# Where the second half of one projection stands among the heads that it feeds: a reordered stretch of a two-block transformer kernel

## The chip, the cores and the metric

The program runs on one core of a Trainium2 chip. The metric is the device time of one execution in microseconds. Before the change it was 1682.24 us, the median of three runs (1674.70 to 1685.97 us). Engines: PE is TensorE, DVE is VectorE, ACT is ScalarE, POOL is GpSimd, SP is SyncE, which only issues transfers here.

## The reference

Two blocks follow each other on one sequence of 256 tokens of width 2048, all in fp32. The first is an attention and recurrent block with a modulated norm; the change doesn't touch it. The second mixes three branches, multiplies them by one matrix, and ends in a feed-forward part:

```python
h = rms_norm(x, g_mix[l])
z = h @ w_in[l]
z_pool, z_q, z_kv, z_kr, z_mq = jnp.split(z, IN_SPLITS_2, axis=-1)
y_pool = pool_mixer(z_pool, w_pool[l], pool_scale[l])
y_mla = mla_mixer(z_q, z_kv, z_kr, pos, ...)            # 8 heads, keys and values from a latent of 256
y_mem = memory_cross_attention(z_mq, mem, ...)          # 4 heads over 256 memory rows
x = x + jnp.concatenate([y_pool, y_mla, y_mem], axis=-1) @ w_o[l]
x = x + conv_glu_ffn(rms_norm(x, g_ffn[l]), w_gate[l], w_up[l], conv_w[l], conv_b[l], w_down[l])
```

Each of the 8 heads of `mla_mixer` takes 192 query and key columns from up-projections of the latents, norms them, rotates 64 of them, and does a causal softmax over 256 keys and the product with 128 value columns.

## The kernel before

**Blocks and halves.** Activations lie transposed, 128 features by 256 tokens to a tile. Every fp32 weight is split into two parts of fp32r: ScalarE copies the hi part (`wh`, L1366), VectorE subtracts it for the low part (`wl`, L1748). A block is one 128 x 128 piece of weight; it takes three matmuls of 256 columns (L1077 to L1079). Eight blocks are a half; its weights come as half of a 1 MB transfer into one of 4 `raw` buffers, and `wh` and `wl` have four slots each. TensorE starts a half when its low part is there (`s_lo`), and ScalarE fills a slot when the half four before is done (`s_half`). So each half costs ScalarE and VectorE one instruction of 128 x 1024.

**The order.** `plan()` lists the weight blocks as the host packs them, `order()` the same blocks with the small work between. The small work (head tasks) is given to six lanes. After each block `step()` may issue the next stage of a lane if the planner's own clocks say that its input is there; `until(...)` and `force` issue stages at once, whatever the clocks say. Every engine then runs its part of the one list in order: an instruction that waits holds up all behind it on its engine.

**Names in the stretch.** For the mla heads g is 0 (heads 0 to 3) or 1 (heads 4 to 7). `un` are the key projections, one tile a head, `uq` the query projections, `ur` the rotary parts of two heads, and `uv` the values of four heads, a tile of its own kind (`m_half`: the activations are the stationary side, L1100 to L1102, and it fills two banks). `oa`, `ob` and `o2` are the output matrix in three parts by rows: `oa` (four blocks a tile, 16 tiles) needs the cross-attention heads, `ob` (six blocks a tile) heads 0 to 3 and the pool groups 0 and 1, `o2` heads 4 to 7 and the pool groups 2 and 3. Each tile is added into `xs` by VectorE (L2166). `pz` are the pool branch's projections, which GpSimd averages (L2305 to L2313), and `pf` the small products behind them (`pool_end`, L1341, scaled by L2178).

**A head's stages**, in order: sq (squares on ScalarE, L1592 to L1598), rot (L1306), u (L2058, L2267, L2270), ss (sums of squares, L1310 to L1312), r1 (L1752), rstd (L1558, L1560), norm (L2007 to L2011, L2064, L2065 on VectorE and then L2274, L2278 on GpSimd), scores (L1235), max (L1939, L1942), exp (L1496), rc (L1945), scale (L1500), turn (L1242), pt (L1504), pv (L1246, L1248), hi (L1608), lo (L2070). Heads h and h + 4 use the same buffers, and the hook `scored` on `un`, `uq` and `ur` forces the stages of head h up to its scores before the tile of head h + 4 is copied:

```python
def scored(tile):
    h = 2 * tile[1] + 1 if tile[0] == "ur" else tile[1]
    if h >= 4:
        o.until((("mla", h - 4), "scores"))
    o.plain(tile)
```

**Banks.** Tiles take the PSUM banks 0 to 3 in turn, and the first matmul of a tile waits until the tile before it in that bank is copied or added (`bank_clear`).

**Values.** `vv` and `vx` hold 256 x 512 values each. `vx` has the cross-attention values first; before the change it also takes the values of heads 4 to 7 (L1627), once the four cross heads are through (L1631 to L1633), and the pv of a head reads `(vv, vx)[h // 4]` (L1320).

Of the kernel before, what the change touches and what calls it, by code (L numbers as in the profile page):

```python
# [14 lines left out]
P = 128  # L15
T = 256
D = 2048
KT = D // P
# [87 lines left out]
def plan():  # L106
# [46 lines left out]
    ups = []  # L153
# [21 lines left out]
    for name, kts in O2_PARTS:  # L175
        blocks = [("w_o_2", kt, (128 * j,)) for j in range(KT) for kt in kts]
        parts.append([blocks[i:i + 8] for i in range(0, len(blocks), 8)])
    line += tile_halves(128) + parts[0] + ups[1]["un"] + ups[1]["uv"] + ups[1]["uq"] + ups[1]["ur"] + tile_halves(256) + tile_halves(384)
    line += parts[1] + parts[2]
    for u in range(0, len(line), 2):  # L180
        out.append(("x", "second", line[u] + line[u + 1]))
    for j in range(FT):
# [275 lines left out]
def order():  # L458
# [256 lines left out]
    heads(0)  # L715
    pool_tile(1)
    o.until(*[("mem", j) for j in range(4)])
    o2_part(0, 0, KT)
    up(1, ("un", "uq", "ur", "uv"))
    heads(1)  # L720
    pool_end(0, o.gemm_bank())
    pool_end(1, o.gemm_bank())
    pool_tile(2)
    pool_tile(3)
    o.mix_half = o.half
    pool_end(2, o.gemm_bank())
    pool_end(3, o.gemm_bank())
    o.until(*[("mla", h) for h in range(4)])
    o2_part(1, 0, KT)
    o.until(*[("mla", h) for h in range(4, 8)])  # L730
    o2_part(2, 0, KT)
    o.o2_half = o.half
# [44 lines left out]
def program(nc, table, wts, ada, xN, xT, memN, cb, cst, vec, msk, wpool, dt, out):  # L777
    o = order()
    with ExitStack() as ctx:
# [283 lines left out]
        def _(e):  # L1063
# [234 lines left out]
            def mla(t, k):  # L1298
                h = t[1]
                s = h % 4  # L1300
                B, bank, j = lset[s], 4 + s, h // 2
                half = slice(64 * (h % 2), 64 * (h % 2) + 64)
                q, kh, qrh = qn[:, s, :], kn[:, s, :], qr[half, j % 2, :]
                if k == "rot":
                    e.wait_ge(*after(t, "act", "gr"))
                    e.matmul(ps[bank][:, 0:T], cs[half, CST["rot"][0]:CST["rot"][1]], qrh, start=True, stop=True).then_inc(mark(t, "pe", "rot"))  # L1306
                if k == "ss":
                    e.wait_ge(*after(t, "dve", "u"))
                    e.wait_ge(*after(("rk",), "act", "sq"))
                    e.matmul(ps[bank][:, :], ones[:], B["sq"], start=True, stop=False)  # L1310
                    e.matmul(ps[bank][:, 0:T], ones[half, :], B["r"][half, 0:T], start=False, stop=False)
                    e.matmul(ps[bank][:, T:512], ones[half, :], krr[half, :], start=False, stop=True).then_inc(mark(t, "pe", "ss"))  # L1312
                if k in SOFTMAX:
                    if k == "scores":
                        e.wait_ge(*after(t, "dve", "k"))
                        e.wait_ge(*after(t, "pool", "kr"))
                    if k == "pv":
                        e.wait_ge(*after(("uv", h // 4), "act", "c1"))
                    softmax(t, k, bank, [(q, kh), (qrh, B["sq"][half, 0:T])], True,
                            [(vv, vx)[h // 4][:, i, s * P:(s + 1) * P] for i in range(2)], B)  # L1320

            def cross(t, k):
                h = t[1]
# [37 lines left out]
        def _(e):  # L1361
# [262 lines left out]
                    e.activation(hB[:, 12 + h, 0:T], ps[4 + lane][:, 0:T], ACT.Copy).then_inc(mark(t, "act", "hi"))  # L1624

            def m_tile(t):
                dst = {"mk": lambda: kraw.rearrange("p (a b) -> p a b", a=2), "mv": lambda: vx, "uv": lambda: (vv, vx)[t[1]]}[t[0]]()  # L1627
                e.wait_ge(*tile_end(t))
                if t[0] in ("mk", "mv"):
                    e.wait_ge(*after(("open",), "dve", "mr4"))  # L1630
                if t == ("uv", 1):  # L1631
                    for h in range(4):
                        e.wait_ge(*after(("mem", h), "pe", "pv"))  # L1633
                banks = o.banks[t]
                for i in range(2):
                    scale = rmc[:, i:i + 1] if t[0] in ("mk", "mv") else 1.0
                    e.activation(dst[:, i, :], ps[banks[i]][:, :], ACT.Copy, scale=scale).then_inc(mark(t, "act", f"c{i}"))
# [796 lines left out]
```

## Time and profile before

| what | value |
|---|---|
| median of three runs | 1682.24 us |
| the profiled execution | 1685.97 us |
| its span, first to last instruction | 1684.2 us |
| mean granted TensorE clock | 0.981 |
| PE busy | 1605.6 us (95%) |
| DVE busy | 1171.0 us (70%) |
| ACT busy | 876.0 us (52%) |
| POOL busy | 130.6 us (8%) |
| the profile's chain that ended last | PE 77%, DVE 12%, ACT 6%, issue 3%, POOL 2% |

The span is what the profile's times refer to. Busy times of PE include modelled ends of pipelined matmuls, so one matmul's duration is longer than the distance to the next. The stretch that the change reorders lies between 757 and 890 us.

### The profile page before, as it was taken

The numbers are of one execution on the slowest core, as the hardware profiler recorded it, in microseconds if no ns is written. First come the engines' busy times: TensorE is split into PE (matmuls) and PEld (weight loads), VectorE is DVE, ScalarE is ACT, GpSimd is POOL, SyncE is SP. The second block draws the span as 40 slices with busy tenths as digits, with TensorE's granted clock in tenths as the row PEclk, the third lists the DMA queues.
The fourth block names the chain that finished last, engine by engine and source line by source line (L and its number), as shares of the span: only waits on it lengthen the run. The fifth ranks groups of instructions, "written<-read, shape, count | busy, mean of one in ns | idle before, by whom it ended". The sixth has DMA issues, their size and how long they took to land.

```text
span 1684.2 us, 25128 instructions
## 1 busy us (share of the span) xinstructions
PE 1605.6 (95%) x9962; PEld 1426.1 (85%) x9962; DVE 1171.0 (70%) x1758; ACT 876.0 (52%) x1362; POOL 130.6 (8%) x151
## 2 busy tenths in 40 slices
PE   6979899989998999988999999999999999999998
PEld 5767789988998999986899888888888888887887
DVE  4778776877676986657586777777777767556554
ACT  7654545767654555463555554444444444444442
POOL 0000000321210220022413000000000000000000
PEclk9989999999999999998999999999999999999999
DMA  8789975533455774342244455554555455555552
GB/s 323 294 336 375 349 299 197 204 113 108 175 200 196 286 276 175 128 148 76 101 145 152 166 189 178 197 191 175 185 200 178 174 198 198 177 188 187 200 177 74
DMA packets 48869, 332.14 MB, mean 197 GB/s; under 512 B 5424, under 2 KB 8880, under 8 KB 9072
## 3 DMA queue, kind: packets, MB, share of 16 engines
q1 hardware_dynamic: 48384, 328.17, 53.5%
q0 software_dynamic: 368, 2.36, 0.4%
q8 instruction: 79, 1.29, 0.3%
q14 instruction: 38, 0.31, 0.1%
HBM read 328.41 MB, written 2.10 MB: 196 GB/s over the span
## 4 chain that ended last, share of the span: by engine, by line
PE 77%; DVE 12%; ACT 6%; issue 3%; POOL 2%; DMA 0%; ACTq 0%; SPq 0%; DVEq 0%; POOLq 0%
PE ps L1081 29%; PE ps L1082 15%; PE ps L1077 7%; PE ps L1079 6%; PE ps L1078 6%; DVE wl L1748 3%; DVE raw L1784 3%; ACT wh L1366 3%; PE ps L1124 2%; PE ps L1126 2%; PE ps L1125 2%; DVE xs L2166 1%; PE ps L1160 1%; PE ps L1161 1%; PE ps L1202 1%
## 5 line engine op out<-in xcount | busy, mean ns | idle before, releaser
L1748 DVE TENSOR_TENSOR wl<-raw,wh 128x1024 fp32r<-128x1024 f32 x512 | 625.0, 1233 | 376.8 <-ACT wh L1366 375.9
L1366 ACT ACTIVATE wh<-raw 128x1024 fp32r<-128x1024 f32 x512 | 530.2, 1054 | 375.9 <-PE ps L1082 172.8
L1081 PE MATMUL ps<-hA,wh 128*128 128x512 f32 x1408 | 499.2, 400 | 0.0
L1082 PE MATMUL ps<-hA,wl 128*128 128x256 f32 x1408 | 396.2, 281 | 0.0
L1081 PEld LDWEIGHTS ps<-hA,wh 128*128 128x128 f32 x1408 | 265.3, 188 | 66.2
L1082 PEld LDWEIGHTS ps<-hA,wl 128*128 128x128 f32 x1408 | 266.7, 189 | 0.0
L1081 PE MATMUL ps<-hB,wh 128*128 128x512 f32 x704 | 250.1, 398 | 2.4 <-DVE xs L2166 1.5
L1077 PE MATMUL ps<-hA,wh 128*128 128x256 f32 x752 | 221.3, 294 | 0.0
L1078 PE MATMUL ps<-hA,wh 128*128 128x256 f32 x752 | 213.3, 284 | 0.0
L1079 PE MATMUL ps<-hA,wl 128*128 128x256 f32 x752 | 213.1, 283 | 0.0
L1082 PE MATMUL ps<-hB,wl 128*128 128x256 f32 x704 | 198.1, 281 | 0.0
L1077 PE MATMUL ps<-hB,wh 128*128 128x256 f32 x576 | 168.0, 292 | 12.4 <-DVE hB L1927 6.6
L1078 PE MATMUL ps<-hB,wh 128*128 128x256 f32 x576 | 164.4, 285 | 0.0
L1079 PE MATMUL ps<-hB,wl 128*128 128x256 f32 x576 | 164.3, 285 | 0.0
L1081 PEld LDWEIGHTS ps<-hB,wh 128*128 128x128 f32 x704 | 132.1, 188 | 37.5 <-DVE xs L2166 3.4
L1077 PEld LDWEIGHTS ps<-hA,wh 128*128 128x128 f32 x752 | 144.5, 192 | 1.8 <-issue 1.2
L1078 PEld LDWEIGHTS ps<-hA,wh 128*128 128x128 f32 x752 | 144.7, 192 | 0.8 <-issue 0.2
L1079 PEld LDWEIGHTS ps<-hA,wl 128*128 128x128 f32 x752 | 144.6, 192 | 0.0
L1082 PEld LDWEIGHTS ps<-hB,wl 128*128 128x128 f32 x704 | 132.7, 189 | 0.0
L1077 PEld LDWEIGHTS ps<-hB,wh 128*128 128x128 f32 x576 | 111.3, 193 | 17.4 <-issue 14.3
L1124 PE MATMUL ps<-wh,hA 128*128 128x512 f32 x256 | 103.3, 403 | 19.4 <-ACT xs L1543 7.1
L1078 PEld LDWEIGHTS ps<-hB,wh 128*128 128x128 f32 x576 | 111.4, 193 | 0.4 <-issue 0.2
(277 smaller groups left out, 2000.0 us busy)
## 6 DMA issues: line engine op xcount, KB each, us to landing
raw<-in_wts SPq DMA_DIRECT2D x256, 1024.0 KB, 4.8
raw<-in_ada SPq DMA_DIRECT2D x48, 1024.0 KB, 5.1
work<-in_memN SPq DMA_DIRECT2D x2, 1024.0 KB, 7.5
xs<-in_xN SPq DMA_DIRECT2D x1, 2048.0 KB, 22.2
xs<-in_xT POOLq DMA_DIRECT2D x2, 1024.0 KB, 5.7
out_T<-xs SPq DMA_DIRECT2D x16, 128.0 KB, 1.7
work<-in_cb SPq DMA_DIRECT2D x1, 1024.0 KB, 14.3
wp<-in_dt SPq DMA_DIRECT2D x8, 128.0 KB, 2.3
```

Source lines behind the costliest of these rows:

```text
L1077: e.matmul(po, w1, hl[:, 0:T], start=first, stop=False)
L1078: e.matmul(po, w1, hl[:, T:2 * T], start=False, stop=False)
L1079: i = e.matmul(po, w2, hl[:, 0:T], start=False, stop=last)
L1081: e.matmul(ps[bank][:, :], w1, hl, start=first, stop=False)
L1082: i = e.matmul(ps[bank][:, T:2 * T], w2, hl[:, 0:T], start=False, stop=last)
L1124: e.matmul(po, hi, w1, start=kt == kts[0], stop=False)
L1125: e.matmul(po, hi, w2, start=False, stop=False)
L1126: m = e.matmul(po, lo, w1, start=False, stop=kt == kts[-1])
L1160: e.matmul(po, hi, w1, start=kt == 0, stop=False)
L1366: e.activation(wh[:, h % WS, :], raw[:, n % RAW, part * HALF:(part + 1) * HALF], ACT.Copy).then_inc(s_hi)
L1748: e.tensor_tensor(wl[:, h % WS, :], src, wh[:, h % WS, :].bitcast(F32), ALU.subtract).then_inc(s_lo)
L1784: e.tensor_tensor_reduce(src, src, cbt, 1.0, 0.0, ALU.mult, ALU.add, c).then_inc(mark(t, "dve", "ttr"))
```

## The change

The second group's keys and queries (`un`, `uq`, `ur` of heads 4 to 7) come after eight of the sixteen `oa` tiles instead of after all; the other eight `oa` tiles follow, and then the second group's values (`uv` 1), after heads 0 to 3 are through. The values go into `vv`, in place of those of heads 0 to 3, and no longer into `vx`; so their copy waits for the pv of head 3 and no longer for the cross heads. The pool products `pf` 2 and 3 come behind four tiles of `ob` instead of ahead of them. The wait for heads 0 to 3 now stands ahead of `uv` 1 instead of ahead of `ob`. `plan()` packs the weights in the new order.

```diff
@@ plan()
-    line += tile_halves(128) + parts[0] + ups[1]["un"] + ups[1]["uv"] + ups[1]["uq"] + ups[1]["ur"] + tile_halves(256) + tile_halves(384)
-    line += parts[1] + parts[2]
+    line += tile_halves(128) + parts[0][:4]
+    for key in ("un", "uq", "ur"):
+        line += ups[1][key]
+    line += parts[0][4:] + ups[1]["uv"] + tile_halves(256) + tile_halves(384) + parts[1] + parts[2]
@@ order()
     o.until(*[("mem", j) for j in range(4)])
-    o2_part(0, 0, KT)
-    up(1, ("un", "uq", "ur", "uv"))
+    o2_part(0, 0, 8)
+    up(1, ("un", "uq", "ur"))
+    o2_part(0, 8, KT)
+    o.until(*[("mla", h) for h in range(4)])
+    up(1, ("uv",))
     heads(1)
     pool_end(0, o.gemm_bank())
     pool_end(1, o.gemm_bank())
     pool_tile(2)
     pool_tile(3)
     o.mix_half = o.half
+    o2_part(1, 0, 4)
     pool_end(2, o.gemm_bank())
     pool_end(3, o.gemm_bank())
-    o.until(*[("mla", h) for h in range(4)])
-    o2_part(1, 0, KT)
+    o2_part(1, 4, KT)
@@ TensorE, mla()
-                            [(vv, vx)[h // 4][:, i, s * P:(s + 1) * P] for i in range(2)], B)
+                            [vv[:, i, s * P:(s + 1) * P] for i in range(2)], B)
@@ ScalarE, m_tile()
-                dst = {"mk": lambda: kraw.rearrange("p (a b) -> p a b", a=2), "mv": lambda: vx, "uv": lambda: (vv, vx)[t[1]]}[t[0]]()
+                dst = {"mk": lambda: kraw.rearrange("p (a b) -> p a b", a=2), "mv": lambda: vx, "uv": lambda: vv}[t[0]]()
                 if t == ("uv", 1):
-                    for h in range(4):
-                        e.wait_ge(*after(("mem", h), "pe", "pv"))
+                    e.wait_ge(*after(("mla", 3), "pe", "pv"))
```

What the planner makes of it, at two places. The first is VectorE at the norms of heads 0 to 3. Before, from the norm of head 3 (its five rows from L2007 to L2065) to the start of that of head 0; `xs<-xs,ps` is the add of an `oa` tile, `wl<-raw,wh` the low part of a half:

```order
L2007 TENSOR_TENSOR ps<-work 128x512
L2009 SCALAR_TENSOR_TENSOR ps<-ps,work 128x512
L2011 SCALAR_TENSOR_TENSOR work<-ps,work 128x512
L2064 SCALAR_TENSOR_TENSOR work<-work,cols 128x256
L2065 SCALAR_TENSOR_TENSOR work<-work,vs 128x256
L2166 TENSOR_TENSOR xs<-xs,ps 128x256
L1748 TENSOR_TENSOR wl<-raw,wh 128x1024
L2166 TENSOR_TENSOR xs<-xs,ps 128x256 x2
L1748 TENSOR_TENSOR wl<-raw,wh 128x1024
L2166 TENSOR_TENSOR xs<-xs,ps 128x256
L2007 TENSOR_TENSOR ps<-work 128x512
```

Now, with lines four higher, from the low part ahead of the second pair of rotations on (r1 and the norm of head 2, and at once that of head 3):

```order
L1752 TENSOR_TENSOR wl<-raw,wh 128x1024
L2062 TENSOR_TENSOR work<-ps,cs 64x256 x2
L1756 TENSOR_SCALAR work<-ps 128x512 x2
L2011 TENSOR_TENSOR ps<-work 128x512
L2013 SCALAR_TENSOR_TENSOR ps<-ps,work 128x512
L2015 SCALAR_TENSOR_TENSOR work<-ps,work 128x512
L2068 SCALAR_TENSOR_TENSOR work<-work,cols 128x256
L2069 SCALAR_TENSOR_TENSOR work<-work,vs 128x256
L2011 TENSOR_TENSOR ps<-work 128x512
L2013 SCALAR_TENSOR_TENSOR ps<-ps,work 128x512
L2015 SCALAR_TENSOR_TENSOR work<-ps,work 128x512
```

The low parts and the adds that stood between the norms are gone from there; they follow behind the norm of head 1.

The second place is VectorE at the scaling of the pool products 2 and 3 (L2178, now L2182). Before, behind the norm of head 6:

```order
L2007 TENSOR_TENSOR ps<-work 128x512
L2009 SCALAR_TENSOR_TENSOR ps<-ps,work 128x512
L2011 SCALAR_TENSOR_TENSOR work<-ps,work 128x512
L2064 SCALAR_TENSOR_TENSOR work<-work,cols 128x256
L2065 SCALAR_TENSOR_TENSOR work<-work,vs 128x256
L1752 TENSOR_SCALAR work<-ps 128x512
L2178 TENSOR_SCALAR work<-ps,vs 128x256
```

Now, behind those of heads 4 and 7:

```order
L2011 TENSOR_TENSOR ps<-work 128x512
L2013 SCALAR_TENSOR_TENSOR ps<-ps,work 128x512
L2015 SCALAR_TENSOR_TENSOR work<-ps,work 128x512
L2068 SCALAR_TENSOR_TENSOR work<-work,cols 128x256
L2069 SCALAR_TENSOR_TENSOR work<-work,vs 128x256
L2170 TENSOR_TENSOR xs<-xs,ps 128x256
L2011 TENSOR_TENSOR ps<-work 128x512
L2013 SCALAR_TENSOR_TENSOR ps<-ps,work 128x512
L2015 SCALAR_TENSOR_TENSOR work<-ps,work 128x512
L2068 SCALAR_TENSOR_TENSOR work<-work,cols 128x256
L2069 SCALAR_TENSOR_TENSOR work<-work,vs 128x256
L2182 TENSOR_SCALAR work<-ps,vs 128x256
```

Two norms and the add of `ob` 3 stand directly ahead of the scaling, where one norm stood.

## Rows read from the trace of the kernel before

**Rows 1.** The page: busy us (share) x instructions; a group: busy us, mean ns

```profile
PE 1605.6 (95%) x9962; PEld 1426.1 (85%) x9962; DVE 1171.0 (70%) x1758; ACT 876.0 (52%) x1362; POOL 130.6 (8%) x151
L1748 DVE TENSOR_TENSOR wl<-raw,wh 128x1024 fp32r<-128x1024 f32 x512 | 625.0, 1233 | 376.8 <-ACT wh L1366 375.9
```

**Rows 2.** Windows: length, busy us (instructions) by engine, granted clock, DMA share, GB/s

```profile
771.00:778.00 7.00, 6.75 (x54) 6.21 (x52) 6.83 (x12) 3.11 (x4) 2.95 (x4) 1.00 0.28 118
778.00:786.00 8.00, 5.80 (x35) 4.31 (x35) 7.86 (x18) 2.21 (x3) 2.34 (x3) 1.00 0.39 131
786.00:801.00 15.00, 13.16 (x43) 9.77 (x44) 8.34 (x26) 6.26 (x21) 1.75 (x2) 0.54 0.00 1
...
838.00:845.00 7.00, 6.78 (x40) 5.22 (x40) 5.13 (x8) 3.44 (x6) 3.22 (x5) 1.00 0.21 44
845.00:885.00 40.00, 39.86 (x311) 37.21 (x309) 32.39 (x67) 21.09 (x44) 5.33 (x6) 1.00 0.41 151
```

**Rows 3.** Timeline of PE: start, us, instruction, [idle before <- releaser]

```profile
778.39 0.39 PE L1077 MATMUL ps<-hB,wh 128*128 128x256 f32 x1 [0.63 <-DVE xs L2166]
785.99 3.00 PE L1235 MATMUL ps<-work 128*128 128x128 f32 x8 [1.81 <-POOL work L2278]
792.40 3.20 PE L1235 MATMUL ps<-work 128*128 128x128 f32 x8 [1.84 <-POOL work L2278]
838.22 0.70 PE L1341 MATMUL ps<-work,wp 128*128 128x256 f32 x2 [1.83 <-POOL work L2313]
885.72 0.55 PE L1242 MATMUL ps<-cs,work 128*128 128x128 f32 x3 [0.86 <-ACT work L1500]
886.94 0.67 PE L1246 MATMUL ps<-work 128*128 128x256 f32 x2 [0.67 <-ACT work L1504]
888.82 0.39 PE L1077 MATMUL ps<-hB,wh 128*128 128x256 f32 x1 [0.64 <-DVE hB L2070]
```

**Rows 4.** PE's pace: chain of waits (0.12, 0.21, 0.43, 0.23) and timeline (the rest)

```profile
760.08 0.12 PE ps L1078
...
760.60 0.70 PE L1306 MATMUL ps<-work,cs 64*128 64x256 f32 x4
761.23 1.12 PE L1310 MATMUL ps<-work,ones 128*128 128x512 f32 x2
...
763.34 1.13 PE L1310 MATMUL ps<-work,ones 128*128 128x512 f32 x2
...
779.21 3.37 PE L1235 MATMUL ps<-work 128*128 128x128 f32 x16
...
796.54 0.21 PE ps L1077
...
798.88 0.43 PE ps L1101
...
800.31 0.23 PE ps L1102
```

**Rows 5.** Timeline of the other engines at a head's stages, and the pool products

```profile
764.90 0.63 ACT L1560 ACTIVATE work<-work 128x512 f32<-128x512 f32 x1
...
781.72 0.69 DVE L2007 TENSOR_TENSOR ps<-work 128x512 f32<-128x512 f32 x1
...
785.05 0.79 POOL L2278 TENSOR_TENSOR work<-work 64x256 f32<-64x256 f32 x1
785.18 0.28 DVE L1939 CUSTOM_DVE_ANT_0 work<-ps,cs 128x128 f32<-128x128 f32 x1
...
785.85 0.17 DVE L1942 TENSOR_SCALAR cols<-cols 128x2 f32<-128x2 f32 x1
...
801.97 1.09 ACT L1637 ACTIVATE work<-ps 128x512 f32<-128x512 f32 x2 [2.14 <-PE ps L1102]
...
812.60 1.03 PE L1341 MATMUL ps<-work,wp 128*128 128x256 f32 x4
```

## The prediction

> **What bounds the kernel now.** I read the page first: the engines' busy shares and the costliest groups [rows 1]. TensorE is busy for 1605.6 of 1684.2 us, so only 79 us of waits are to be had in the whole program, and every weight still needs its hi part on ScalarE and its low part on VectorE. The change keeps every matmul and moves only where some of them stand. So the question is which waits of TensorE lie in the moved part, and whether the moved blocks cover more or less of them.
>
> Next the windows from 757 to 890 us [rows 2]. Between 771 and 786 us VectorE is nearly full (6.83 of 7 and 7.86 of 8 us), and from 786 to 801 us the granted clock is 0.54: most of it runs at 1.2 instead of 2.4 GHz. Then the timeline of TensorE [rows 3]. In the moved part it waits 0.63, 1.81 and 1.84 us for the scores of heads 0 and 1 (from VectorE or, through it, GpSimd), 1.83 us for the pool branch, and 0.86, 0.67 and 0.64 us for the end of head 5: 8.3 us in all. That is the ceiling of what the move can save in waits; what the clock costs comes on top.
>
> **The pace of the blocks.** One matmul of a block takes 0.12 us of TensorE at full clock and 0.21 at half [rows 4]. A half (eight blocks of three) is therefore 24 x 0.119 (rounded to 0.12 in the rows) = 2.86 us. The four halves of oa 8 to 15 that the change takes out from in front of un 4 are worth 11.4 us of cover. Both orders are alike up to the end of oa 7. The rotations of heads 0 and 1 stand at 760.6 us behind six blocks of oa 8 and 9 [rows 4]; six blocks are 2.1 us, so oa 7 ends at 758.4 us in both.
>
> **Part 1: scores 0 to 3 with less cover.** The planner's hook at un 4 forces everything up to scores 0, the hook at un 5 scores 1. Before, this is spread over four halves; now it stands in one row behind two blocks of un 4, which end at 759.1 us. The pieces: the sums of squares cost TensorE 2.1 us a head (761.23 to 763.34) [rows 4]; from their end to a finished rstd it is 2.2 us (763.34 to 765.53); a head's norm is 3.5 us on VectorE (781.72 to 785.18), and from its start to the start of the scores 4.3 us (781.72 to 785.99), since GpSimd's two multiplications follow; a head's max is 0.8 us [rows 3, 5]. Scores cost 1.65 us at full clock (3.37 for two heads) and 3.0 to 3.2 at half [rows 3, 4].
>
> Step by step, at full clock: rotations to 760.5, four sums of squares to 768.9. The first rstd input is ready at 762.7, the second at 764.8; norm 2 runs from 765.5, norm 3 from 769.0; then two rstd inputs, max 2 and max 3 (held until scores 3 end at 775.0) up to 776.0; norm 0 from 776.0, norm 1 from 779.5. Scores start at 769.8, 773.3, 780.3 and 783.8 and end at 785.5. Before, the same point is 795.6 us, with 11.4 us more work done: 784.2 like for like. So the loss is only 1.3 us, although four halves are gone, because VectorE's row lost its riders: the low halves (1.23 us each) and the adds of oa 8 to 15 [rows 5] no longer stand between the norms.
>
> Now the clock. Before, the second half of the low stretch, after 795.6 us, costs about 2.0 us: 12 matmuls at 0.21 for 0.12, and four of the m tile at 0.43 for 0.23 [rows 4]. If the clock stays high now, this part is 1.3 - 2.0 = -0.7 us. If it falls before scores 0, as I expect from waits of about 2 and 5 us in a row, scores 0 end at 783.3, un 5 at 784.6, scores 1 at 787.7 (+2.2), and what follows runs 2 to 5 us at half speed (+1.0 to +2.6, I take 1.5): +3.0. The bounds are -0.7 and +4.1.
>
> Rows 3 and 2 show both answers: waits of 1.81 and 1.84 us stand in a low stretch, a wait of 1.83 us at 838 us in one with a granted clock of 1.00. The Trainium skill, "TensorE: Matmul & The Clock Gate", section "HAM oscillation", says that waits between short bursts let the clock fall, so that the next burst starts cold; it speaks against this change, which makes one long gap of several short ones. By that rule this part is the +3.0; by the row at 838 us alone it would be -0.7.
>
> **Part 2: uv 1 behind the heads, into vv.** Its copy on ScalarE now waits for head 3's pv instead of the cross heads'. Head 3's pv stands over four halves ahead of it (11 us), so the wait costs nothing. But uv 1 is now directly ahead of the pool blocks, and pz 2 takes a bank of uv 1: it waits for a 1.09 us copy, covered by two pool products, 1.03 us with the tail of the last and some 0.7 without [rows 5]. With the 0.2 us from matmul to copy that leaves +0.6 us (0 to 1.3). If ScalarE were still busy with a hi part (1.05 us) it would be the 1.3. Heads 4 to 7 wait for uv 1 only at their pv, a dozen halves later.
>
> **Part 3: the pool products pf 2 and pf 3, four tiles later.** The 1.83 us at 838 us goes: -1.8, since GpSimd has three halves (8.6 us) more. What is late next: pf 2 stands on VectorE behind the norms of heads 4 and 7, two times 3.5 us, where before only one norm stood ahead of it, and ob 6 takes the bank of pf 2. From the end of ob 3 TensorE has the two products (0.7 us) and ob 4 and ob 5 (12 blocks, 4.3 us) before it, 5.0 in all; VectorE, which by the same count starts the first norm 0.7 us before the end of ob 3, has 7.0 + 0.4 (the add of ob 3) + 0.4, so it is there after 7.1. That would be a wait of 2.1 us; since the start of that norm is the least sure of these, I take half, +1.0 (0 to 2.1). No DMA moves: each load stays tied to its half.
>
> **Part 4: the end of heads 4 to 7.** Before, all of head 5 from scale to low part is forced after ob 15: 0.86 + 0.67 + 0.64 = 2.17 us [rows 3]. Now its turn stands ahead of the last block and its transposed copy beside head 4's pv, so only the wait for the low part stays, some 0.9 us: -1.3 (-2.2 to 0).
>
> **The sum**, from the profiled execution: +3.0 + 0.6 - 1.8 + 1.0 - 1.3 = +1.5 us. That execution took 1685.97 us (the span of 1684.2 and 1.8 around it), so it would be 1687.5; it was the slowest of three, and the median is 1682.24. On the median the forecast is 1683.7 us. About 1% (17 us) is what a measurement of this kernel can tell from no change; every wait in the moved part together is half of that.
>
> **The rivals.**
> First, the clock holds through the row of waits. The 1.00 around 838 us speaks for it, the low stretch at 786 us against it. Part 1 becomes -0.7, the sum -2.2 us: 1680.0. If the whole tail of head 5 is covered as well and ob 6 doesn't wait, it is -0.7 + 0.6 - 1.8 - 2.2 = -4.1: 1678.1. This is faster than before.
> Second, slower than before by more than I say: VectorE falls behind from ob 2 on. Three norms (heads 6, 4 and 7) now stand within two halves, and the low halves wait behind them. I count some 0.8 us to spare before a low half is late for TensorE. One further norm of lag (3.5 us) would give 2.7 us there and 3.5 more at ob 6, and head 5's end would keep its 2.2: 1.5 + 2.7 + 3.5 + 1.3 = +9.0, 1691.2. It decides from a scale of pf 2 that ends over 8 us after the end of ob 3 (7.1 in my count). For it: VectorE's 7.86 of 8 us in the like stretch; against: behind the stretch, between 845 and 885 us, it was busy 32.39 of 40 us [rows 2] and had room to catch up.
> Third, the order does not act: where TensorE waits is set by the heads' chains, whose total is unchanged, so waits move and the sum is 0: 1682.2. That four parts of up to 3 us meet near zero looks like this too, but each would be seen at its own place.
>
> **How the numbers follow.** Forecast 0.50, the clock holds 0.22, VectorE falls behind 0.15, nothing moves 0.13. The cases reach from 1678.1 to 1691.2. The three times of before spread from 1674.7 to 1686.0, 7.5 us below and 3.7 above their median, and the new median carries such a spread, so the range is 1674.0 to 1691.5. Faster by over 1% (below 1665.4) needs twice all waits of the part: 0.03. Slower by over 1% (above 1699.1) needs the second rival twice over: 0.03. Within 1%: 0.94.
>
> **What would show it.** In the new timeline: waits of about 2 and 5 us ahead of the scores near 773 and 780 us, scores 1 done at 785 to 788 us instead of 795.6; a low granted clock some 10 us earlier than before; no wait ahead of the second pair of pool products, and one of 1 to 2 us behind the next two tiles (12 blocks); one wait near the end of ob 15 in place of three. Wrong would be: a wait of over 3 us anywhere behind uq 4, a VectorE wait of TensorE for a low half (that line's wl) between 835 and 880 us, or a difference of over 10 us.

## The result, and the profile after

The changed kernel takes 1688.86 us, the median of 20 executions (1681.38 to 1701.69), the kernel before 1683.34 beside it. The ratio is 1.0066 [1.0046, 1.0087], some 11 us slower; two of the 20 executions of the kernel before took 3150 us and don't count in it. The forecast was +1.5 us, so the sign was right and the size was not. The profiled execution of the changed kernel took 1687.06 us (span 1685.3), that of before 1685.97. Those two differ by 1 us only. The difference of 11 us is not in their totals, so where it hides has to be found first.

The engines' busy times of the page after:

```profile
PE 1602.1 (95%) x9962; PEld 1428.4 (85%) x9962; DVE 1172.1 (70%) x1758; ACT 876.2 (52%) x1362; POOL 134.1 (8%) x151
```

The counts are those of [rows 1], so no work came or went. TensorE is even 3.5 us less busy. The costliest group of its matmuls tells why: it lies far behind the change, in the feed-forward part. Before:

```profile
L1081 PE MATMUL ps<-hA,wh 128*128 128x512 f32 x1408 | 499.2, 400 | 0.0
```

After:

```profile
L1086 PE MATMUL ps<-hA,wh 128*128 128x512 f32 x1408 | 489.9, 395 | 0.0
```

The same 1408 matmuls took 9.3 us less in this execution, and the kernel before, run a second time with nothing changed, shows 489.9 us as well. So this differs between executions of one kernel without any change, and it hid the change's price in the profiled pair. (These matmuls overlap, so their busy time is no sum of costs. The elapsed time of that part is given with the experiments.)

So I measure a stretch between two fixed instructions that holds everything the change moves: from the first rotation of head 2 to the sum of squares of the second rms norm. In the timeline of TensorE, before:

```profile
753.03 0.70 PE L1306 MATMUL ps<-work,cs 64*128 64x256 f32 x4
...
928.52 0.70 PE L1283 MATMUL ps<-work,ones 128*128 128x256 f32 x2 [2.18 <-POOL work L2289]
```

After, with every wait of TensorE of more than 0.25 us between the same two:

```profile
754.87 0.70 PE L1311 MATMUL ps<-work,cs 64*128 64x256 f32 x4
...
770.98 1.74 PE L1240 MATMUL ps<-work 128*128 128x128 f32 x8 [0.80 <-POOL work L2282]
...
774.96 3.20 PE L1240 MATMUL ps<-work 128*128 128x128 f32 x8 [2.24 <-POOL work L2282]
...
783.21 3.19 PE L1240 MATMUL ps<-work 128*128 128x128 f32 x8 [5.05 <-POOL work L2282]
...
822.32 0.36 PE L1082 MATMUL ps<-hA,wh 128*128 128x256 f32 x1 [0.40 <-ACT work L1641]
...
856.43 3.20 PE L1240 MATMUL ps<-work 128*128 128x128 f32 x8 [5.43 <-POOL work L2282]
...
869.69 0.39 PE L1082 MATMUL ps<-hB,wh 128*128 128x256 f32 x1 [0.48 <-DVE work L2182]
...
941.00 0.70 PE L1288 MATMUL ps<-work,ones 128*128 128x256 f32 x2 [2.25 <-POOL work L2293]
```

The stretch went from 175.5 us (928.52 - 753.03) to 186.1 (941.00 - 754.87): +10.6 us. That is the 11 us of the ratio. Its waits went from 10.5 us ([rows 3] with the 2.18 above) to 16.7. The waits that are new stand at two places: the row of three at the scores of heads 2, 3 and 0, which the prediction walked through, and 5.43 us ahead of the scores of head 6, which it doesn't name. The windows after, which answer to [rows 2]:

```profile
774.00:795.00 21.00, 14.99 (x50) 11.07 (x51) 11.84 (x35) 8.71 (x25) 4.28 (x5) 0.52 0.00 1
...
850.00:857.00 7.00, 1.57 (x10) 1.37 (x9) 3.32 (x5) 3.46 (x5) 5.82 (x7) 0.74 0.36 124
857.00:864.00 7.00, 7.00 (x29) 5.70 (x29) 3.25 (x10) 0.00 (x0) 0.01 (x1) 0.53 0.06 26
```

The low clock (1.2 GHz) lasts 20.5 us now, from 774.8 to 795.3 us (granted 0.52), where it was 13.7 us; and it falls a second time, for 10.2 us, in the wait that ends at 856 us (0.74 and 0.53). In the window from 850 to 857 us TensorE is busy 1.57 of 7 us, VectorE 3.32 and GpSimd 5.82 of 7: the engine that is busy there is the one with 8% of the span on the page.

The timeline of GpSimd after shows what it did (norm of head 6: L2278 and L2282):

```profile
834.12 3.71 POOL L2309 TENSOR_TENSOR work<-work 128x256 f32<-128x256 f32 x3 [47.06 <-DVE work L2139]
...
845.12 3.14 POOL L2309 TENSOR_TENSOR work<-work 128x256 f32<-128x256 f32 x4
...
850.72 0.72 POOL L2271 TENSOR_TENSOR work<-work,cs 64x256 f32<-64x256 f32 x1
...
852.31 1.59 POOL L2271 TENSOR_TENSOR work<-work,cs 64x256 f32<-64x256 f32 x1
...
854.78 0.72 POOL L2278 TENSOR_TENSOR work<-work 64x256 f32<-64x256 f32 x1
855.57 0.72 POOL L2282 TENSOR_TENSOR work<-work 64x256 f32<-64x256 f32 x1
```

From 834.12 to 856.3 us it never stands idle for longer than 0.1 us: first `pz` 2 and the rotary multiplications (u) of heads 6 and 7, then `pz` 3 (845.12 to 850.64) and those of heads 4 and 5, and behind them the two multiplications of head 6's norm. VectorE had finished its part of that norm long before:

```profile
849.57 0.48 DVE L2069 SCALAR_TENSOR_TENSOR work<-work,vs 128x256 f32<-128x256 f32 x1
```

So head 6's last stage was ready for GpSimd at about 850 us and started at 854.78. Before, GpSimd began `pz` 2 at 823.72 us and head 6's norm came out at 841.5 us, ahead of its scores at 843.60, which did not wait:

```profile
823.72 0.61 POOL L2305 TENSOR_TENSOR work<-work 128x256 f32<-128x256 f32 x1 [0.30 <-DVE work L2135]
...
832.85 3.28 POOL L2305 TENSOR_TENSOR work<-work 128x256 f32<-128x256 f32 x4
...
840.74 0.80 POOL L2278 TENSOR_TENSOR work<-work 64x256 f32<-64x256 f32 x1
```

GpSimd's order is nearly the old one: `pz` 3 and the rotary stage of head 5 stood ahead of head 6's norm before as well. Only two items moved: the rotary stage of head 6, which was ahead of `pz` 2, is behind it, and that of head 4, which was ahead of `pz` 3, is behind that. What changed is the time. Counted from the first matmul of `pz` 2 on TensorE (813.27 us before, 822.32 after), GpSimd was through with head 6's norm after 28.3 us and is now after 34.0, while TensorE was ready for the scores after 30.3 us and is now after 28.7. So 2.1 us to spare became a wait of 5.4.

Of GpSimd's 5.7 us, 4.35 are a longer row: 17.82 us from the start of `pz` 2 to the end of the norm before, 22.17 after, with one head's rotary stage more in it and with some single instructions slower (1.59 us for 0.72 at the same size). The other 1.35 us are a later start, and they show on ScalarE, at the first instruction of each head (its squares). Before, the first two heads start at 816.32 and 817.79 us, and the other two wait until a head of the first group has left its lane (releaser: that head's low part):

```profile
824.02 0.42 ACT L1592 ACTIVATE work<-work 128x256 f32<-128x256 f32 x1 [2.68 <-DVE hB L2070]
...
830.67 0.42 ACT L1592 ACTIVATE work<-work 128x256 f32<-128x256 f32 x1 [2.13 <-DVE hB L2070]
```

After, heads 0 to 3 are all through ahead of `uv` 1, every lane is free, and the four start behind it at 824.64, 826.10, 827.81 and 829.29 us without a wait. The next hi part stands behind all four of them on ScalarE. VectorE waits 6.10 us for it, and the add of `pz` 2 stands behind its low part:

```profile
824.64 0.40 ACT L1597 ACTIVATE work<-work 128x256 f32<-128x256 f32 x1
...
829.29 0.40 ACT L1597 ACTIVATE work<-work 128x256 f32<-128x256 f32 x1
...
831.00 2.95 ACT L1371 ACTIVATE wh<-raw 128x1024 fp32r<-128x1024 f32 x3
...
832.09 1.23 DVE L1752 TENSOR_TENSOR wl<-raw,wh 128x1024 fp32r<-128x1024 f32 x1 [6.10 <-ACT wh L1371]
833.23 0.42 DVE L2116 TENSOR_TENSOR work<-ps,work 128x256 f32<-128x256 f32 x1
```

So GpSimd starts on `pz` 2 6.0 us behind its last matmul (834.12 against 828.1), where it was 2.7 (823.72 against 821.0). VectorE's wait goes with the number of heads in the row: 3.32 us before with two, 4.37 in e4 below with three, 6.10 with four. No run changes that number alone.

TensorE is ready 1.6 us earlier mostly by what moved away: the two pool products with their wait (835.69 to 838.57 us, 2.9) and 1.65 us of work for heads 0 and 1 no longer stand between `pz` 2 and the scores of head 6, while nine more blocks of `ob` do (3.2 us).

### The profile page after: what moved, and what is told of

The parts are those of the page before. It is cut to its first block, busy times and chain, and to the rows that moved or that the text cites. A ratio compares the mean times of both kernels' runs of the same rounds, so it can differ in the third digit from the quotient of the medians.

```text
span 1685.3 us, 25127 instructions
## 1 busy us (share of the span) xinstructions
PE 1602.1 (95%) x9962; PEld 1428.4 (85%) x9962; DVE 1172.1 (70%) x1758; ACT 876.2 (52%) x1362; POOL 134.1 (8%) x151
## 4 chain that ended last, share of the span: by engine, by line
PE 75%; DVE 11%; ACT 6%; issue 3%; POOL 2%; DMA 2%; ACTq 0%; SPq 0%; DVEq 0%; POOLq 0%
PE ps L1086 28%; PE ps L1087 14%; PE ps L1082 7%; PE ps L1083 6%; PE ps L1084 6%; DVE wl L1752 3%; ACT wh L1371 3%; PE ps L1129 3%; PE ps L1130 2%; PE ps L1131 2%; DVE raw L1788 2%; DMA raw<-in_wts 1%; PE ps L1240 1%; DVE xs L2170 1%; PE ps L1207 1%
## 5 line engine op out<-in xcount | busy, mean ns | idle before, releaser
L1086 PE MATMUL ps<-hA,wh 128*128 128x512 f32 x1408 | 489.9, 395 | 0.0
```

The costliest lines, as they stand in the source:

```text
L1086: e.matmul(ps[bank][:, :], w1, hl, start=first, stop=False)
```

## The experiments

Theory: two losses, the row at `un` 4 (part 1) and GpSimd's queue in front of the scores of head 6. Rivals: VectorE behind, the placing of `pf` 2 and 3, and the values of heads 4 to 7 by themselves. For the last there is no run of its own; the trace after shows 0.40 us of wait at a bank of `uv` 1 and none of TensorE at the pv of heads 4 to 7. "Stretch" is the one above, in the profiled execution of each; "waits" are TensorE's idle times of over 0.25 us in it; "low" is the time in it at 1.2 GHz.

| kernel | stretch us | waits us | low us | ratio to before |
|---|---|---|---|---|
| before | 175.5 | 10.5 | 13.7 | 1 |
| before again | 175.5 | 10.5 | 13.7 | |
| after | 186.1 | 16.7 | 30.7 | 1.0066 [1.0046, 1.0087] |
| after again | 186.0 | 16.7 | 30.7 | |
| e1: after, GpSimd's order | 179.5 | 13.1 | 20.5 | 1.0008 [0.9969, 1.0046] |
| e2: after, `pf` as before | 191.0 | 21.9 | 34.1 | 1.0115 [1.0050, 1.0181] |
| e3: before, `pf` late | 177.1 | 12.8 | 10.2 | 1.0016 [0.9983, 1.0049] |
| e4: after, 12 `oa` tiles first | 178.3 | 11.6 | 20.5 | 1.0019 [0.9984, 1.0055] |
| e5: after, own buffers | 172.5 | 8.8 | 10.2 | 0.9975 [0.9945, 1.0005] |
| e5 again | 172.1 | 8.8 | 10.2 | 0.9980 [0.9952, 1.0008] |
| e6: e5 with e1 | 171.3 | 10.0 | 3.4 | 0.9952 [0.9924, 0.9979] |
| e7: e3 with e1 | 176.6 | 11.7 | 13.7 | 0.9980 [0.9948, 1.0011] |
| e8: e4 with e1 | 178.2 | 13.0 | 17.1 | 1.0007 [0.9982, 1.0032] |
| e9: before, queries first | 184.7 | 17.3 | 20.5 | 1.0018 [0.9992, 1.0045] |

**e1, GpSimd's order.** The changed kernel, with one item moved in GpSimd's instructions alone: `pz` 3 goes behind the norm of head 6.

```diff
-            for b in o.beats:
+            line = list(o.beats)
+            line.remove(("ev", ("pz", 3)))
+            line.insert(line.index(("t", ("mla", 6), "norm")) + 1, ("ev", ("pz", 3)))
+            for b in line:
```

> The changed kernel, but on GpSimd alone the work of pool group 3 stands behind the norm of head 6 instead of ahead of the rotations of heads 4 and 5. The stretch is read from the first rotation matmul of head 2 to the ones-matmul of the second rms norm: 175.5 us before, 186.4 us after the change. Theory 1 (GpSimd's queue: its work for pool group 3 and two rotations stood ahead of the norm of head 6, so scores 6 waited 5.4 us and the clock fell): the wait ahead of scores 6 falls to under 1 us, the low clock near 853 us goes, pf 3 waits about 1 us, the stretch is 180 to 182 us, and the kernel is 4 to 6 us faster than the changed one. Theory 2 (VectorE falls behind from ob 2 on): scores 6 waits as long, the stretch stays at 186 us. Theory 3 (the shorter cover at un 4 is the whole loss, the later wait only moved there): the wait turns up again within the next two halves, stretch 185 to 187 us.

The stretch fell by 6.6 us, to 179.5, a little below the 180 to 182 of theory 1. The waits of part 1 stood as they were (0.80, 2.25, 5.05), and the big one was gone. TensorE:

```profile
850.71 1.74 PE L1240 MATMUL ps<-work 128*128 128x128 f32 x8 [0.56 <-POOL work L2282]
...
856.82 0.70 PE L1346 MATMUL ps<-work,wp 128*128 128x256 f32 x2 [1.25 <-POOL work L2317]
```

and GpSimd, which now waits for VectorE ahead of the norm and does `pz` 3 behind it:

```profile
848.74 0.96 POOL L2278 TENSOR_TENSOR work<-work 64x256 f32<-64x256 f32 x1 [1.03 <-DVE work L2015]
...
850.64 3.68 POOL L2309 TENSOR_TENSOR work<-work 128x256 f32<-128x256 f32 x4
```

The scores take 1.74 us instead of 3.20, since the clock no longer fell. That one place in GpSimd's queue is 6.6 of the 10.6 us is shown by this run: nothing else was touched. The place itself is not new; the change made it count.

**e2, `pf` back, and e3, `pf` late on its own.** e2 is the changed kernel with the pool products where they were; e3 the kernel before with only these moved.

```diff
 (e2, on after)
-    o2_part(1, 0, 4)
     pool_end(2, o.gemm_bank())
     pool_end(3, o.gemm_bank())
-    o2_part(1, 4, KT)
+    o2_part(1, 0, KT)
 (e3, on before)
-    pool_end(2, o.gemm_bank())
-    pool_end(3, o.gemm_bank())
     o.until(*[("mla", h) for h in range(4)])
-    o2_part(1, 0, KT)
+    o2_part(1, 0, 4)
+    pool_end(2, o.gemm_bank())
+    pool_end(3, o.gemm_bank())
+    o2_part(1, 4, KT)
```

> The changed kernel with pf 2 and 3 ahead of ob 0 again; all other instructions stand as in the changed kernel. Theory 1 (GpSimd's queue): pf 3 now waits for pool group 3, whose work ends at 850.6 us where TensorE is there at 841 us: a wait of 8 to 10 us at pf 3, and a remaining one of 2 to 5 us at scores 6; stretch 187 to 191 us. Theory 2 (the place of pf is what costs, because its scaling stands behind two norms on VectorE): the stretch falls by 1 to 3 us, to 184 or 185 us.

> The kernel before with only the last part of the change: pf 2 and 3 behind four tiles of ob. Theory 1: the 1.83 us wait at pf 3 goes and nothing takes its place but under 1 us at a bank; stretch 173 to 174.5 us (before 175.5), time 0 to 2 us less than before. Theory 2 (the place of pf costs): a wait of 1 to 3 us for the scaling, stretch 176 to 178 us.

e2 was slower by 4.9 us in the stretch, and 1.0115 [1.0050, 1.0181] in the ratio:

```profile
839.54 1.22 PE L1345 MATMUL ps<-work,wp 128*128 128x256 f32 x2 [4.23 <-POOL work L2316]
...
847.74 1.22 PE L1345 MATMUL ps<-work,wp 128*128 128x256 f32 x2 [6.97 <-POOL work L2316]
```

The products wait 11.2 us for GpSimd in place of the scores of head 6, which don't wait now. The stretch and the sum of waits are near what theory 1 said, though it put 2 to 5 us of them at head 6; theory 2 is out. So moving `pf` late is a repair inside the change, not its fault: GpSimd is late for something in either order. At the old place of the products it is late by 11.2 us, where it was by 1.83 before.

e3 took 177.1 us, 1.6 more than before. Theory 1 had said less than before; the time lies in theory 2's range, but the wait is not the one for the scaling that it gave as the reason.

```profile
786.02 1.74 PE L1236 MATMUL ps<-work 128*128 128x128 f32 x8 [1.81 <-POOL work L2279]
...
792.44 2.88 PE L1236 MATMUL ps<-work 128*128 128x128 f32 x8 [3.77 <-POOL work L2279]
...
842.15 1.74 PE L1236 MATMUL ps<-work 128*128 128x128 f32 x8 [1.70 <-POOL work L2279]
```

The 1.83 us of the pool product [rows 3] did not go; 1.70 of it turned up at the scores of head 6, which wait for the same GpSimd. So on the kernel before this part of the change brings nothing. The first two rows tell something else. The scores of head 0 ran at full clock here (1.74 us for 3.00 before, behind the same wait of 1.81), and those of head 1 started at the same time as before, 792.44 for 792.40, with a longer wait (3.77 us for 1.84): head 1's norm sets that start, and a faster TensorE only waits longer.

**e4, more cover at `un` 4.** Twelve `oa` tiles ahead of the second group's projections in place of eight.

```diff
-    line += tile_halves(128) + parts[0][:4]
+    line += tile_halves(128) + parts[0][:6]
-    line += parts[0][4:] + ups[1]["uv"] + tile_halves(256) + tile_halves(384) + parts[1] + parts[2]
+    line += parts[0][6:] + ups[1]["uv"] + tile_halves(256) + tile_halves(384) + parts[1] + parts[2]
-    o2_part(0, 0, 8)
+    o2_part(0, 0, 12)
-    o2_part(0, 8, KT)
+    o2_part(0, 12, KT)
```

> The changed kernel with 12 oa tiles ahead of un 4 in place of 8, so 2.5 halves less of cover are taken away. By the walk of the norms on VectorE the waits ahead of scores 0 to 3 fall from 8.1 to about 3 to 5 us, and the low clock there from 20 to 10 to 14 us. Theory 1 (two separate losses): pool group 2 starts 2 to 3 us earlier like for like, but the wait ahead of scores 6 stays at 3 to 6 us, since GpSimd's order is the same; stretch 182 to 184 us. Theory 3 (all is the cover at un 4): the wait at scores 6 shrinks with it, stretch 178 to 181 us.

178.3 us: 7.8 less than after. The row of waits became 2.63 and 2.29 us for 0.80, 2.24 and 5.05, and the wait at head 6 shrank to 4.04 us:

```profile
780.53 2.82 PE L1240 MATMUL ps<-work 128*128 128x128 f32 x8 [2.63 <-POOL work L2282]
...
785.64 3.20 PE L1240 MATMUL ps<-work 128*128 128x128 f32 x8 [2.29 <-POOL work L2282]
...
847.80 3.20 PE L1240 MATMUL ps<-work 128*128 128x128 f32 x8 [4.04 <-POOL work L2282]
```

Two halves of cover (5.7 us by the pace of [rows 4]) took 3.2 us from the waits there and 10.2 us from the time at 1.2 GHz in the whole stretch. Cover is what the row lacked, as part 1 says. The stretch is in the range of theory 3, not of theory 1: the wait at head 6 shrank with the row. So the two losses are not separate, since the planner's order around `pz` 3 changes with the cover (three heads start in a row, and the rotary stage of head 4 is ahead of `pz` 3, as before the change). It still is not faster than the kernel before.

**e5 and its repeat, own buffers.** The test of part 1 by itself: the row exists because heads h and h + 4 share buffers. Here heads 4 to 7 have their own (keys in `vx`, which the change left free, queries in `kx`, the rotary part in another free buffer), so nothing is forced at `un` 4 and after; the order of the weight blocks stays, but the planner spreads the head work anew over all of the stretch.

```diff
-        if h >= 4:
-            o.until((("mla", h - 4), "scores"))
         o.plain(tile)
...
+        qr1 = work[:, a1 - 2 * T:a1].rearrange("p (a b) -> p a b", a=2)
+        kn1 = vx.rearrange("p a b -> p (a b)").rearrange("p (a b) -> p a b", a=4)
+        kns, qns, qrs = (kn, kn1), (qn, kx), (qr, qr1)
...
-                    dst = kn[:, j % 4, :] if name == "un" else qn[:, j % 4, :] if name == "uq" else qr[:, j % 2, :]
-                    if name != "ur" and j >= 4:
-                        e.wait_ge(*after(("mla", j - 4), "pe", "s"))
-                    if name == "ur" and j >= 2:
-                        e.wait_ge(*after(("mla", 2 * (j - 2) + 1), "pe", "s"))
+                    g = j // 2 if name == "ur" else j // 4
+                    dst = kns[g][:, j % 4, :] if name == "un" else qns[g][:, j % 4, :] if name == "uq" else qrs[g][:, j % 2, :]
+                    if (name, j) in (("un", 4), ("uq", 4), ("ur", 2)):
+                        for h in range(4):
+                            e.wait_ge(*after(("mem", h), "pe", "pv"))
```

> The changed kernel, but the keys, queries and rope parts of heads 4 to 7 get buffers of their own (the memory values' and keys' buffers and two of the cross queries'), so that nothing is forced at un 4 to ur 3. This takes away what the waits ahead of scores 2, 3 and 0 (0.8 + 2.2 + 5.1 us) and the low clock of 20 us there come from. Theory A (they come from the short cover at un 4): these waits shrink to under 2 us in all and the low clock there goes; some 1 to 4 us come back in front of uv 1, where the tails of heads 0 and 1 are forced; the wait ahead of scores 6 stays at 4 to 6 us. Stretch 178 to 181 us (changed kernel 186.1). Rival (VectorE's total work in these 20 us sets the end, wherever TensorE waits): the same 8 us turn up at uv 1, stretch 184 to 187 us.

> The version with buffers of their own for heads 4 to 7 once more, to time it against the kernel before in more rounds. Stretch 172.5 us again within 1.5 us (the clock's low stretches can fall elsewhere), 3 us below the kernel before; total 2 to 6 us below it, a ratio of 0.997 to 0.999.

172.5 and 172.1 us: 14 us less than after and 3 less than before, and well below the 178 to 181 expected. The window that holds the row now has no low clock and hardly a wait (42.27 of 43 us busy):

```profile
757.00:800.00 43.00, 42.27 (x279) 34.07 (x277) 35.28 (x70) 22.99 (x51) 13.26 (x15) 1.00 0.33 119
```

What is left are 1.48 and 0.67 us at the pv of the tail ahead of `uv` 1, and 4.04 us at head 6, as in e4:

```profile
800.75 0.67 PE L1252 MATMUL ps<-work 128*128 128x256 f32 x2 [1.48 <-ACT work L1510]
...
840.70 3.20 PE L1241 MATMUL ps<-work 128*128 128x128 f32 x8 [4.04 <-POOL work L2283]
```

In the total it is 0.9975 [0.9945, 1.0005], and 0.9980 [0.9952, 1.0008] the second time: each interval ends just above 1.

**e6, own buffers and GpSimd's order.** Both repairs.

> The version with buffers of their own for heads 4 to 7 (stretch 172.5 us, a wait of 4.0 us left ahead of scores 6), and on GpSimd pool group 3 behind the norm of head 6. If GpSimd's queue is the last thing there: the 4.0 us go, stretch 168 to 170 us. If the adds behind two norms on VectorE are next in line, as in the two kernels with 12 tiles and with pf late, a bank wait of 2 to 4 us takes the place: stretch 171 to 173 us. I expect the second.

171.3 us, and 0.9952 [0.9924, 0.9979]: the one kernel here whose interval lies below 1, by half a percent, with a median of 1675.41 us. But GpSimd's order brought 1 us here, not the 6.6 of e1, as the second case of the expectation said. What came in its place:

```profile
848.53 0.55 PE L1083 MATMUL ps<-hB,wh 128*128 128x256 f32 x1 [4.79 <-DVE xs L2171]
```

With head 6 in time, TensorE is through `ob` 3 and the products early and waits for a bank, whose add (L2171) stands on VectorE behind the norms of heads 4 and 7.

**e7 and e8, GpSimd's order with the other two.** The same edit as e1 on e3 and on e4.

> The kernel before with pf 2 and 3 behind four tiles of ob, and on GpSimd pool group 3 behind the norm of head 6. With pf late alone the stretch was 177.1 us: the wait of 1.8 us at pf 3 had gone to scores 6 (1.7 us). GpSimd's queue as the cause: the wait ahead of scores 6 goes, at pf 3 nothing over 1 us comes, stretch 174 to 176 us. Rival (the norm of head 6 on VectorE is itself late, GpSimd's queue costs nothing there): 177 us as before.

> The changed kernel with 12 oa tiles ahead of un 4, and on GpSimd pool group 3 behind the norm of head 6. With the 12 tiles alone the stretch was 178.3 us and the wait ahead of scores 6 4.0 us, with the order on GpSimd alone 179.5 us. If the two losses are separate they add: 186.1 - 7.8 - 6.6 plus what is shared; scores 6 wait under 1 us, and the stretch is 172 to 175 us, below the kernel before (175.5). If GpSimd's order only moves its wait elsewhere: 176 to 179 us.

e7 gives 176.6 us, e8 178.2, against 177.1 and 178.3 without: nothing. The losses of e8 don't add up to the 172 to 175 us that separate ones would give. In both the wait at head 6 went and VectorE's came, 2.99 us in e7:

```profile
853.57 0.36 PE L1078 MATMUL ps<-hB,wh 128*128 128x256 f32 x1 [2.99 <-DVE xs L2167]
```

and 4.79 us in e8, at the same bank.

VectorE of e8, from the start of the norm of head 4 to the add that TensorE waits for:

```profile
848.76 0.78 DVE L2011 TENSOR_TENSOR ps<-work 128x512 f32<-128x512 f32 x1
...
851.83 1.22 DVE L2011 TENSOR_TENSOR ps<-work 128x512 f32<-128x512 f32 x1
...
855.82 1.74 DVE L1752 TENSOR_TENSOR wl<-raw,wh 128x1024 fp32r<-128x1024 f32 x1
857.49 0.74 DVE L2170 TENSOR_TENSOR xs<-xs,ps 128x256 f32<-128x256 f32 x2
```

Two norms and a low part stand ahead of it, 848.76 to 857.49 us, and no idle time is shown ahead of any of these rows. So behind the `pz` blocks two engines are late one behind the other, and what one repair gives depends on how late the other is. In the kernel after, only 0.48 us was left at that bank; that the 5.43 us for GpSimd gave VectorE the time to catch up fits this, but e1 shows that it is not all: there the wait for GpSimd is down to 0.56 and 1.25 us, and the bank costs 0.61.

**e9, queries first.** The other order with less storage: the kernel before, with the queries and rotary parts of heads 4 to 7 in buffers of their own and ahead of the keys, so that they cover what the keys wait for. The order, without the edits for the buffers:

```diff
-    line += tile_halves(128) + parts[0] + ups[1]["un"] + ups[1]["uv"] + ups[1]["uq"] + ups[1]["ur"] + tile_halves(256) + tile_halves(384)
+    line += tile_halves(128) + parts[0] + ups[1]["uq"] + ups[1]["ur"] + ups[1]["un"] + ups[1]["uv"] + tile_halves(256) + tile_halves(384)
-    up(1, ("un", "uq", "ur", "uv"))
+    up(1, ("uq", "ur"))
+    up(1, ("un", "uv"))
...
```

> The kernel before, but the queries and rope parts of heads 4 to 7 have buffers of their own and come ahead of their keys, so that the forced row at un 4 has three halves (8.6 us) more of cover in front of it. Theory A (waits and low clock at un 4 come from too little cover): the waits of 1.8 and 1.8 us ahead of scores 0 and 1 and the low clock there go, the stretch is 168 to 171 us (before 175.5), unless the tail of heads 4 to 7 grows: then 171 to 173 us. Rival (VectorE's work sets the end): the waits only move behind un 4, 175 us.

184.7 us, wrong by far. The waits ahead of the keys did not go (0.64, 0.96, 0.79 and 2.20 us), and GpSimd is late for the pool product:

```profile
835.63 1.22 PE L1344 MATMUL ps<-work,wp 128*128 128x256 f32 x2 [6.01 <-POOL work L2318]
```

The start of the heads is spread here as it is before (813.6, 821.5, 823.7 and 828.8 us), so the four heads in a row are not the only way to make GpSimd late. It has idle gaps in this run and begins `pz` 3 at 830.69 us, 1.4 us behind VectorE's add; its row of 4.9 us for `pz` 3 then lies bare, since the planner put no head work between `pz` 3 and its product. The run shows that buffers for the queries alone, with another order, don't do what e5 does.

**e10 and e11, before and after again.** Unchanged, for the certainty of the stretch.

> The kernel before, unchanged, for the spread of the stretch between executions: the same waits within 0.1 us, the low clock within 7 us of before's place, and 175.5 us within 1.5 us. The part behind the stretch can differ by 10 us: it was 738 us in some profiles and 748 in others.

> The changed kernel, unchanged, for the spread of the stretch: waits of 5.0 us ahead of scores 0 and 5.4 us ahead of scores 6 again, and 186 us within 2 us.

175.51 and 185.99 us for 175.49 and 186.13: the stretch repeats to 0.2 us. The low clock falls at the same matmuls too: before it begins at 786.2 us in one and at 790.3 in the other, but the stretch begins 4.1 us later there (757.17 for 753.03), with 13.7 us of it in both. The scores of head 0, before again, take 3.04 us for 3.00:

```profile
790.12 3.04 PE L1235 MATMUL ps<-work 128*128 128x128 f32 x8 [1.81 <-POOL work L2278]
```

From the end of the stretch to the last matmul the kernel before took 749.3 us in one execution and 740.4 in the other, and over all kernels here it is either 736 to 741 or 745 to 750. This spread of some 9 us is as large as the whole effect, and it is why only a dozen executions or the stretch can tell these kernels apart.

## Why the prediction was wrong

**Part 3 is the step that failed.** It said "-1.8, since GpSimd has three halves (8.6 us) more", and then put the question "What is late next" to VectorE alone. Its step is that GpSimd would be late by the 1.83 us of before, so that three halves cover it, and that nothing else of TensorE's hangs on GpSimd there. For the pool product it came true: its wait is gone and nothing took its place there. But e2 shows that at the old place GpSimd is late by 11.2 us in the new order, and the scores of head 6, whose norm stands right behind `pz` 3 on GpSimd, now come ahead of the products. e3 shows this for the move of `pf` alone: 1.70 of the 1.83 us turned up at these scores on the kernel before. In the changed kernel GpSimd is 5.7 us later, counted from `pz` 2, as the rows above show. The price is 5.43 us of wait, and the half speed from 856.4 to 863.6 us, of which half is lost (3.6): 9.0 us, against nothing in the sum. e1 moves `pz` 3 behind the norm and gives 6.6 us; most of the rest stayed as 0.56 and 1.25 us of other waits. The durations of GpSimd's instructions were all in the trace of before; its queue was not walked.

The bank wait for VectorE at `ob` 6, forecast at +1.0 (0 to 2.1), was 0.48 us after. The mechanism was right: in three of the four runs with GpSimd's order changed, the same wait is 2.99 to 4.79 us (e7, e8, e6), over the bound; in the fourth, e1, it is 0.61. My count let VectorE start the first norm 0.7 us before the end of `ob` 3, and had no low part between the norms and the add (1.74 us in the row of e8).

**Part 1 was right in kind and too small.** The waits were walked out as about 0.9, 2 and 5 us and came as 0.80, 2.24 and 5.05. Scores 1 were to end at 787.7 us; they ended at 790.8, which is 789.0 without the 1.8 us by which this trace is later already at the first row of the stretch. The clock fell as expected. It fell for longer: 20.5 us in place of 13.7, where I had counted on 2 to 5 us of it behind un 5. At the start of `pz` 2, like for like, this kernel is 5.6 us later than before: 822.32 - 1.84 for the offset - 1.65 for head work that before still owes (815.25 to 816.15 and 827.20 to 827.95 us), against 813.27. Without part 2's 0.4 that is +5.2, where the term was +3.0 and its upper bound +4.1. e5 shows that the stretch is 14 us shorter without the row and its clock, but not that the row costs 14: the planner's order is another one there, and what follows gains too (5.43 became 4.04). One reading of part 1's rows was off without entering the sum: the 0.63 us that the prediction counts to the scores is a wait for a bank behind an add (L2166).

The low clock begins at 774.8 us, at the end of the wait of 2.24 us and behind the one of 0.80; the 5.05 us lie inside it. Here the Trainium skill was weighed ("TensorE: Matmul & The Clock Gate", section "HAM oscillation"): waits between short bursts let the clock fall. The rows after agree. e3 shows that one wait does not decide it: behind the same 1.81 us the scores of head 0 ran once at half and once at full clock.

**Part 2** was right: 0.40 us for a forecast of +0.6 (0 to 1.3), released by ScalarE's copy of `uv` 1 (L1641), at the first matmul of `pz` 2.

**Part 4** was a little better than said: all three waits of head 5's end are gone, -2.2, the end of its range, for -1.3.

**The sum as measured**: +5.2 + 0.4 - 1.8 + 0.5 - 2.2 and the missed 9.0 are 11.1 us, against 10.6 in the stretch and 11 in the ratio. Without the missed term it would be +2.1, close to the forecast of +1.5, but by chance: part 1 was 2.2 too small and the other terms together 1.6 too high.

**The rivals.** The clock did not hold, and the order did act. The second rival (VectorE behind by a norm, +9.0) came near the time, but by the wrong engine, which is luck. After, no scale of `pf` 2 was late enough to hold TensorE for more than 0.48 us; in e6 to e8 TensorE does wait for VectorE there.

**The text's own test** named this: "a wait of over 3 us anywhere behind uq 4". It came, 5.43 us, so the sum fails at part 3 and not at a size alone. The range (1674.0 to 1691.5) holds the median of 1688.86, but it takes in all the rivals and the spread of the executions, and the forecast of 1683.7 is 5 us below. On the kernel before's own median beside it, 1683.34, the forecast of +1.5 stands against +5.5 by the medians and +11 by the ratio. The chance of 0.94 for within 1% stands: the interval ends at 0.87%.

What stays open: why the part behind the stretch takes one of two durations, how the 14 us of e5 divide between waits, clock and the new spread of the head work, and why some of GpSimd's instructions take twice the time of others of the same size. None changes what the change costs.

## What to carry to other kernels

When a block moves ahead, list what newly stands in front of each short operation that TensorE waits for, on every engine's queue, also on one that is busy 8% of the span: a share of the page says nothing about 20 us without a gap. An order forced by a shared buffer is better undone by a second buffer than by another place in the order (e5 and e6 against e4). And when two engines are late behind one another, the repair of one may bring nothing (e7 and e8, and 1 us in e6); no run here repaired both. Where the total spreads by as much as the effect, measure between two fixed instructions.

## What the runs showed of the hardware that I had not expected

**Two durations at full clock.** The wide matmuls of the feed-forward part run at one of two paces, with a granted clock of 1.00 in both. The window from 1000 to 1050 us (same columns as [rows 2]), before:

```profile
1000.00:1050.00 50.00, 50.00 (x285) 43.36 (x284) 37.58 (x59) 23.14 (x35) 0.00 (x0) 1.00 0.53 190
```

Before again, the same program:

```profile
1000.00:1050.00 50.00, 50.00 (x291) 44.10 (x290) 38.46 (x59) 24.32 (x36) 0.00 (x0) 1.00 0.53 200
```

285 or 291 matmuls in 50 us of a TensorE that never idles: 2% of pace, with the same DMA share of 0.53. The cause is not known.

**The same wait, another clock.** The kernel before and the kernel after each let the clock fall within 0.4 us of the same place in both of their executions. But it need not be so. e3 has the same instructions as before up to the pool products and the same wait of 1.81 us; from 786 to 793 us its granted clock was 0.98, where before it was 0.51, and it fell 6.6 us later. And e5 and its repeat, one program, were at 1.2 GHz for 10.2 us each at other places: at 802.3 us for 3.4 us and at 839.9 for 6.8 in one, at 839.8 for all of it in the other. A forecast of the clock from the waits alone is good to some microseconds only.
